# Down projection of a two-layer MLP: Strassen's scheme (Winograd's form) for 14 of 16 groups

## The chip, the cores and the metric

One core of a Trainium2 chip runs the whole program. The metric is the device time of one execution in microseconds (us). The engines have their own instruction queues: TensorE (PE in the profile), VectorE (DVE), ScalarE (ACT), GpSimd (POOL) and SyncE (SP), which here only issues DMAs. They wait for each other through semaphores.

## The reference, cut to what matters

The program is one decoder layer for a prompt of 1024 tokens and 8 decode tokens, model width 1024. Only its last part is touched:

```
x1 = LN(alpha * x + m)
y  = LN(alpha * x1 + relu(x1 @ w_up)^2 @ w_down)      # w_up 1024 x 4096, w_down 4096 x 1024
```

All is float32. A product is made exact enough by splitting: each operand is a rounded high part plus a low part (what the rounding left), and a product is three matmuls, high·high + high·low + low·high.

## The kernel before, in words

**Tiling.** The 4096 hidden channels are 32 tiles of 128, taken in 16 groups of two (group g holds tiles 2g and 2g+1; the prediction counts groups 0 to 15). The *up* half of a group has six chunks, three for each tile: a chunk is 344 tokens wide and takes 8 contraction tiles by 3 matmuls, 24 matmuls of 344 columns (`up`, line 1590; all go through `split_product`, line 902). ScalarE applies the relu of a chunk out of one of four PSUM banks (`relu`, L1958). VectorE squares it (L2636). ScalarE writes the high part (L1984), VectorE the low part (L2643).

**The down half.** `down(g)` (line 1623) runs over 8 token tiles and 2 halves of the 1024 output columns. Each of these 16 sums takes 2 hidden tiles by 3 matmuls of 512 columns and goes to one of three PSUM banks (5 to 7). VectorE adds each sum to `x1` in SBUF (L2672). The sum with number d may start when the add of sum d-3 is done. So a group has 96 such matmuls and 16 adds. The weights of a group, 256 x 1024, come by one DMA of 1 MB (L878) into a double buffer; ScalarE makes their high part (L1998) and VectorE their low part (L2703). The 8 decode tokens have their own small product, `down_decode` (L1619).

**Order.** It is written out by hand for each engine. TensorE, for groups 1 to 14: six up chunks of group g, and then the whole down half of group g-1. Group 15 has its up chunks alone; `down_last` then takes the down halves of groups 14 and 15 together, and the final layer norm runs tile by tile beside it. ScalarE and VectorE go through relu, square, high part, low part, adds, and the split of the next up weights (L920 on ScalarE, L926 on VectorE) in a fixed order. GpSimd does nothing from the merge of the branches to the final layer norm, where it applies gain and bias (L2870, L2872).

Of the kernel before, what the change touches and what calls it, by code (L numbers as in the profile page):

```python
# [28 lines left out]
P = 128  # L29
# [4 lines left out]
NB = 8  # L34
# [130 lines left out]
def hybrid_step(nc, x_p, x_s, c_cmp, c_sel, c_win, state, table, w_in, cmp_w, cmp_pos, lb_logits, norm_g,  # L165
                w_br_a, w_br_b, w_out, ln1_g, ln1_b, w_up, w_down, ln2_g, ln2_b, consts, kpos, dbias, before_d,
                y_p, y_s_out, cmp_p, sel_p, win_p, hg_p, cmp_s, sel_s, win_s, hg_s):
    with ExitStack() as ctx:
# [496 lines left out]
        uT = [aT[:, :, :].rearrange("p (j s) t -> p j s t", s=2), view(0, 2, 2, T)]  # L665
        uR = [rounded("hidden0", aT_at, 0, 2, 2, T), rounded("hidden1", arena_at, 0, 2, 2, T)]
        NG = F_FF // (2 * P)
        LAST = [(0, (NG - 2,)), (1, (NG - 2,)), (2, (NG - 2, NG - 1)), (0, (NG - 1,)), (3, (NG - 2, NG - 1)), (1, (NG - 1,))]
# [3 lines left out]
        def last_sum(e, half):  # L672

            return 16 * (NG - 2) + 2 * e + half

# [23 lines left out]
        y_s, y_g, y_out = sem("y_ready_dve"), sem("y_ready_pool"), sem("y_stored")  # L699
        l2_f, l2_g = sem("ln2_factors"), sem("ln2_gained")  # L700
# [54 lines left out]
        def _(sp):  # L755
# [117 lines left out]
            for g in range(NG):  # L873
                if g == 0:
                    sp.wait_ge(f_ps, NQ + 1)
                if g >= 2:
                    sp.wait_ge(dn_ps, 16 * (g - 1))
                sp.dma_start(wdn[:, g % 2], w_down[0, 2 * P * g:2 * P * (g + 1), :].rearrange("(j p) c -> p j c", p=P)  # L878
                             ).then_inc(wd_in[g % 2], 16)
                if g == 0:  # L880
                    sp.wait_ge(x1_s, NQ + 1)
                    sp.dma_start(lng[:, 0, :], ln2_g.to_broadcast([P, D])).then_inc(ln2_in, 16)
                    sp.dma_start(lng[:, 1, :], ln2_b.to_broadcast([P, D])).then_inc(ln2_in, 16)
                for n in range(U_U + WR + 2 * g, U_U + WR + 2 * (g + 1)):
                    if n < len(units):
                        load_unit(n)
            for p, t in enumerate(LN2_ORDER[:NQ]):
                sp.wait_ge(y_g, p + 1)
                dst = y_p[0, P * t:P * (t + 1), :] if t < NQ else y_s_out[:, 0, :]
                sp.dma_start(dst, x1[0:toks(t), t, :]).then_inc(y_out, 16)  # L890
# [73 lines left out]
        def _(pe):  # L964
# [649 lines left out]
            def down_decode(g):  # L1614
                pe.wait_ge(wd_in[g % 2], 16 * (g // 2 + 1))
                pe.wait_ge(sqd_dve, 2 * (g + 1))
                for c in range(4):
                    j, cols = c // 2, slice(512 * (c % 2), 512 * (c % 2 + 1))
                    mm = pe.matmul(PS[32 * c:32 * c + NB, 4, :], ud[:, g % 2, j, :], wdn[:, g % 2, j, cols],  # L1619
# [3 lines left out]
            def down(g):  # L1623
                pe.wait_ge(wdl_dve, g + 1)
                pe.wait_ge(ul_dve, MIXED + 2 * (g + 1))
                u, w = uR[g % 2], wdl[:, g % 2]
                for t in range(NQ):
                    tk = slice(P * t, P * t + P)
                    for half in range(2):
                        d, cols = 16 * g + 2 * t + half, slice(512 * half, 512 * (half + 1))  # L1630
                        if d >= 3:
                            pe.wait_ge(dn_dve, d - 2)
                        split_product(pe, PS[:, 5 + d % 3, :], [u[:, j, 1, tk] for j in range(2)],
                                      [u[:, j, 0, tk] for j in range(2)], [wdh[:, j, cols] for j in range(2)],
                                      [w[:, j, cols] for j in range(2)]).then_inc(dn_ps, 1)
                    if t == 1:
                        down_decode(g + 1)

            def down_last():
                for e, (t, gs) in enumerate(LAST):  # L1640
                    tk = slice(P * t, P * t + P)
                    pe.wait_ge(wdl_dve, gs[-1] + 1)
                    pe.wait_ge(ul_dve, MIXED + 2 * (gs[-1] + 1))
                    gj = [(g, j) for g in gs for j in range(2)]
                    for half in range(2):
                        d, cols = last_sum(e, half), slice(512 * half, 512 * (half + 1))
                        pe.wait_ge(dn_dve, d - 2)
                        split_product(pe, PS[:, 5 + d % 3, :], [uR[g % 2][:, j, 1, tk] for g, j in gj],
                                      [uR[g % 2][:, j, 0, tk] for g, j in gj], [down_high(g, j)[:, cols] for g, j in gj],
# [15 lines left out]
        def _(act):  # L1665
# [288 lines left out]
            def relu(y):  # L1954
# [3 lines left out]
                act.activation(uT[i // 2 % 2][:, i % 2, 0, c0:c0 + cn], PS[:, (y + 2) % 4, 0:cn], ACT.Relu).then_inc(relu_act, 1)  # L1958
# [15 lines left out]
            for i in range(F_FF // P):  # L1974
                g = i // 2
                if g >= 2:
                    act.wait_ge(dn_ps, 16 * (g - 1))
                for y in range(max(3, up_chunks(i - 1)) if i else 3, up_chunks(i)):
                    relu(y)
                if i == 0:  # L1980
                    act.wait_ge(*unit_done(U_U))
                    split_high(act, U_U + 2, up_high(2))
                act.wait_ge(sq_dve, i + 1)
                act.activation(uR[g % 2][:, i % 2, 1, 0:SEQ], uT[g % 2][:, i % 2, 0, 0:SEQ], ACT.Copy).then_inc(uh_act, 1)  # L1984
                if 1 <= i < F_FF // P - 2:
# [914 lines left out]
```

## Time and profile before

| | us |
|---|---|
| median of 3 runs | 2127.62 (2126.48 to 2130.12) |
| the profiled execution's own time | 2127.94 |
| its span | 2126.1 |
| TensorE busy | 2078.1 (98%) |
| VectorE busy | 1039.2 (49%) |
| ScalarE busy | 687.1 (32%) |
| GpSimd busy | 179.6 (8%) |

The span is what the profiler saw between the first and the last instruction; the time of an execution is a little longer. Matmuls are pipelined: in the timeline the start-to-start distance of two matmuls is what TensorE spends on one, not the length shown. The MLP's groups 1 to 15 and the last sums fill the stretch from 1398.6 us to the end.

### The profile page before, as it was taken

To read this page: it belongs to the slowest core of one execution; us is meant where nothing else is said; L and a number is where in the kernel's file an instruction comes from. 1 tells how busy PE (TensorE), PEld (TensorE's weight loads), DVE (VectorE), ACT (ScalarE), POOL (GpSimd) and SP (SyncE) were. 2 spreads that over 40 slices of the span, in tenths; PEclk is the share of its full clock that TensorE was granted. 3 is DMA by queue.
4 is the path that set the end of the run, shared out by engine and by line. 5 is a ranking of instruction groups with operands and counts; after the bars stand their busy time and mean duration, and the time that the engine had idled before them with its cause. 6 is when DMAs were issued, how large, how long until landed. Compare 5 with 4: busy or idle time off the path is not lost.

```text
span 2126.1 us, 33610 instructions
## 1 busy us (share of the span) xinstructions
PE 2078.1 (98%) x14172; PEld 1808.9 (85%) x14172; DVE 1039.2 (49%) x1915; ACT 687.1 (32%) x1345; POOL 179.6 (8%) x180
## 2 busy tenths in 40 slices
PE   8999999999999999999999999999999999999997
PEld 8997777779589999998888876898889888898985
DVE  2126777656633686675111127744434444444447
ACT  3127777755223444452111130121112111122122
POOL 0011000011500222130000000000000000000007
PEclk9999999999999999999999999999999999999999
DMA  9323010247742222123111131121111111111102
GB/s 222 121 66 115 11 51 2 90 157 248 245 153 51 56 62 56 46 65 122 30 50 40 45 114 48 47 75 40 54 46 50 45 45 41 40 60 50 30 20 80
DMA packets 140738, 159.05 MB, mean 75 GB/s; under 512 B 25843, under 2 KB 122444, under 8 KB 135725
## 3 DMA queue, kind: packets, MB, share of 16 engines
q1 hardware_dynamic: 132556, 114.14, 17.6%
q0 software_dynamic: 8032, 42.78, 6.5%
q8 instruction: 112, 1.84, 0.3%
q14 instruction: 38, 0.30, 0.0%
HBM read 141.32 MB, written 19.76 MB: 76 GB/s over the span
## 4 chain that ended last, share of the span: by engine, by line
PE 92%; DVE 3%; ACT 2%; DMA 1%; issue 1%; SPq 0%; POOL 0%; DVEq 0%; ACTq 0%; POOLq 0%
PE PS L902 64%; PE PS L1525 5%; PE PS L1136 3%; PE PS L1116 3%; PE PS L1224 3%; PE PS L1088 2%; PE PS L1090 1%; PE PS L1209 1%; PE PS L1451 1%; PE PS L1619 1%; DMA arena<-in_x_prompt 1%; PE PS L1145 1%; PE PS L1579 1%; PE PS L1394 1%; PE PS L1337 1%
## 5 line engine op out<-in xcount | busy, mean ns | idle before, releaser
L902 PE MATMUL PS<-x_low,w_high_mlp 128*128 128x344 f32 x1056 | 337.7, 320 | 0.0
L902 PE MATMUL PS<-w_down_high,hidden 128*128 128x512 f32 x960 | 308.2, 395 | 0.9 <-DVE w_down_low L2678 0.9
L902 PE MATMUL PS<-x_high,w_low 128*128 128x344 f32 x768 | 245.8, 320 | 0.0
L2672 DVE TENSOR_TENSOR arena<-arena,PS 128x512 f32<-128x512 f32 x244 | 167.4, 687 | 134.9 <-PE PS L902 134.7
L902 PE MATMUL PS<-x_high,w_high_mlp 128*128 128x344 f32 x720 | 229.8, 319 | 0.0
L902 PEld LDWEIGHTS PS<-w_down_high,hidden 128*128 128x128 f32 x960 | 180.0, 188 | 54.3 <-DVE arena L2672 12.0
L902 PE MATMUL PS<-w_down_low,hidden 128*128 128x512 f32 x512 | 200.9, 392 | 0.0
L902 PEld LDWEIGHTS PS<-x_low,w_high_mlp 128*128 128x128 f32 x1056 | 198.2, 188 | 2.6
L902 PE MATMUL PS<-x_low,w_high_hgrn 128*128 128x344 f32 x600 | 191.8, 320 | 0.0
L902 PE MATMUL PS<-x_high_a,w_low 128*128 128x344 f32 x480 | 153.5, 320 | 0.0
L902 PE MATMUL PS<-x_high_b,w_low 128*128 128x344 f32 x468 | 149.6, 320 | 0.0
L902 PEld LDWEIGHTS PS<-x_high,w_low 128*128 128x128 f32 x768 | 144.2, 188 | 0.0
L902 PEld LDWEIGHTS PS<-x_high,w_high_mlp 128*128 128x128 f32 x720 | 135.4, 188 | 1.5 <-issue 0.9
L1680 ACT ACTIVATE arena<-PS 128x344 f32<-128x344 f32 (+1 forms) x105 | 47.9, 458 | 262.4 <-PE PS L902 262.2
L1998 ACT ACTIVATE w_down_high<-arena 128x2048 fp32r<-128x2048 f32 x15 | 28.7, 1916 | 274.9 <-PE PS L902 274.9
L1525 PE MATMUL PS<-arena,wring 128*128 128x344 f32 x384 | 114.7, 452 | 1.2 <-issue 1.2
L902 PEld LDWEIGHTS PS<-w_down_low,hidden 128*128 128x128 f32 x512 | 96.1, 188 | 21.1
L902 PEld LDWEIGHTS PS<-x_low,w_high_hgrn 128*128 128x128 f32 x600 | 113.1, 189 | 0.0
L2870 POOL TENSOR_TENSOR arena<-arena 128x1024 f32<-128x1024 f32 (+1 forms) x8 | 19.6, 2451 | 1103.2 <-ACT arena L2010 1103.2
L926 DVE TENSOR_TENSOR w_low<-wring,w_high_mlp 128x1024 fp32r<-128x1024 f32 x44 | 53.6, 1220 | 109.0 <-ACT w_high_mlp L920 109.0
L1525 PEld LDWEIGHTS PS<-arena,wring 128*128 128x128 f32 x384 | 72.1, 190 | 35.1 <-issue 1.4
L902 PE MATMUL PS<-x_high_a,w_high_hgrn 128*128 128x344 f32 x300 | 101.3, 338 | 0.3 <-issue 0.3
(399 smaller groups left out, 4236.4 us busy)
## 6 DMA issues: line engine op xcount, KB each, us to landing
wring<-in_w_in SPq DMA_DIRECT2D x100, 256.0 KB, 3.3
wring<-in_w_up SPq DMA_DIRECT2D x64, 256.0 KB, 3.3
arena<-in_w_down SPq DMA_DIRECT2D x16, 1024.0 KB, 5.0
arena<-in_x_prompt SPq DMA_DIRECT2D x16, 512.0 KB, 3.6
x_high_kept<-x_high_att SPq DMA_DIRECT2D x1, 4128.0 KB, 13.9
arena<-in_w_out SPq DMA_DIRECT2D x2, 2048.0 KB, 9.6
out<-in_cache_win_kv SPq DMA_DIRECT2D x1, 4088.0 KB
out<-arena SPq DMA_DIRECT2D x7, 512.0 KB
```

The lines of the kernel that those rows point to most:

```text
L902: mm = pe.matmul(out, w, x, start=(start and k == 0 and i == 0), stop=(stop and k == tiles - 1 and i == 2))
L926: dve.tensor_tensor(wl[:, n % WR, :, 0:m], wring[:, n % WR, :, 0:m], high[:, :, 0:m].bitcast(F32), ALU.subtract).then_inc(wl_dve, 1)
L1088: pe.matmul(out, qa, k1[g][:, br, k0:k0 + n], start=True, stop=False)
L1090: mm = pe.matmul(out, qb, k2[br][g][0:65, k0:k0 + n], start=False, stop=True)
L1116: mm = pe.transpose(PS[0:n, 4 + turned % 2, P * b:P * (b + 1)], probs(j, col, n), ident)
L1136: mm = pe.matmul(PS[HD * two:HD * (two + 1), 6 + i % 2, c:c + P], v[0:r, :], PT[(2 * n + two) % 3][0:r, b // 4, P * (b % 4):P * (b % 4 + 1 ...
L1145: mm = pe.transpose(PS[:, 6 + n % 2, P * a:P * (a + 1)], out_parts(n)[:, P * a:P * (a + 1)], ident)
L1224: mm = pe.matmul(PS[:, 4 + 2 * (b % 2) + c, 0:256], cw2[:, c, 4 * half + q, :], xt2[:, n % 2, 256 * (4 * c + q):256 * (4 * c + q + 1)], st ...
L1525: mm = pe.matmul(PS[:, product_bank(s, ab), 0:cn], wring[:, n % WR, 4 * ab + k, :], a[:, k, c0:c0 + cn], start=(k == 0), stop=(k == 3))
L1680: act.activation(dst[0:m, c0:c0 + cn], unit_out(3 * n + ci, m, cn), fn).then_inc(u_act, 1)
L1998: act.activation(wdh[:, :, :], wdn[:, g % 2], ACT.Copy).then_inc(wdh_act, 1)
L2672: dve.tensor_tensor(y, y, PS[:, 5 + d % 3, :], ALU.add).then_inc(dn_dve, 1)
```

## The change

For groups 0 to 13 (`NS` = 14) the down half is computed in 2 x 2 blocks. Token tiles p and p+4 form a pair (p = 0 to 3); the blocks of the left operand are (tile p or p+4) by (hidden tile 2g or 2g+1), those of the right operand (hidden tile) by (512 output columns). Winograd's form of Strassen's scheme needs seven products of blocks instead of eight, and sums of blocks on both sides. For each pair there are four sums of squares of hidden blocks (128 x 128 elements each), for each group four sums of weight blocks (128 x 512 each). GpSimd computes them: 20 `tensor_tensor` instructions a group, in the order pairs 0, 1, 2, weights, pair 3.

A product is three matmuls of 512 columns, so a pair has 21 and a group 84. Four of the seven products have a bank of their own start; the other three (`False` in `PRODUCTS`) go on accumulating in the bank of the product three before, after that one has been added. Each of the seven is added to `x1` by VectorE: six adds of 512 elements a row, and one that adds the same sum to both halves (1024 elements).

TensorE's order in groups 1 to 14: up chunks 0 and 1, the decode product, chunk 2, pair 0 of group g-1, chunk 3, pair 1, chunk 4, pair 2, chunk 5, pair 3. The high and low parts are made of the blocks and of their sums (896 elements a row for a pair, 1536 for the weight blocks, twice 1024 for the weight sums). The buffers are single: relu output, weight parts and weight sums are not double-buffered. The weights of groups 1 to 13 are fetched when the sums, the low parts and the decode product of the group before are done. Groups 14 and 15 are computed as before, with their high parts written after the last Strassen product; the decode product of group 14 moves from the down half in group 14 to group 15, and the loads of the second layer norm's gain and bias from the start of the MLP to before the weights of group 14.

```
+        PRODUCTS = ((1, 0, True), (3, 2, True), (4, 3, True), (6, 4, False), (2, 5, True), (7, 1, False), (5, 6, False))
...
             for g in range(NG):
                 if g == 0:
-                    sp.wait_ge(f_ps, NQ + 1)
-                if g >= 2:
-                    sp.wait_ge(dn_ps, 16 * (g - 1))
...
+                elif g <= NS:
+                    sp.wait_ge(y_g, 4 * g)
+                    sp.wait_ge(wdl_dve, 3 * (g - 1) + 1)
+                    sp.wait_ge(dd_ps, g)
...
+            def down(g, p):
+                pe.wait_ge(ul_dve, MIXED + 4 * g + p + 1)
+                for m, (a, b, first) in enumerate(PRODUCTS):
+                    d = product(g, p, m)
+                    if p == 0 and m in (0, 2, 4):
+                        pe.wait_ge(wdl_dve, 3 * g + m // 2 + 1)
+                    if d >= 3:
+                        pe.wait_ge(dn_dve, d - 2)
+                    for i, (h, w) in enumerate(((hp_high[p][:, a - 1, :], wp_high[:, b, :]), (hp_high[p][:, a - 1, :], part_low(b)),
+                                                (hp_low[p][:, a, :], wp_high[:, b, :]))):
+                        mm = pe.matmul(PS[:, 5 + d % 3, :], h, w, start=(first and i == 0), stop=(i == 2), skip_group_check=True)
+                    mm.then_inc(dn_ps, 1)
...
             for g in range(NG):
                 if g >= 1:
-                    for y in range(6 * g, 6 * g + 6):
-                        up(y)
-                        if y == 8:
-                            down_decode(0)
-                if 1 <= g < NG - 1:
-                    down(g - 1)
+                    for c in range(6):
+                        up(6 * g + c)
+                        if c == 1 and g <= NS or c == 2 and g == NG - 1:
+                            down_decode(g - 1)
+                        if c >= 2 and g <= NS:
+                            down(g - 1, c - 2)
...
+            for g in range(1, NS + 1):            # ScalarE
+                quarters_high(g - 1)
+                parts_high(g - 1, 0)
+                sums_high(g - 1, 0)
+                relu(6 * g)
+                parts_high(g - 1, 1)
+                sums_high(g - 1, 1)
+                parts_high(g - 1, 2)
+                relu(6 * g + 1)
+                parts_high(g - 1, 3)
+                relu(6 * g + 2)
+                up_split(2 * g + 2)
+                for c in range(3, 6):
+                    relu(6 * g + c)
+                up_split(2 * g + 3)
...
+            def square_quarters(g, p):
+
+                dve.wait_ge(relu_act, up_chunks(2 * g + 1))
+                if g:
+                    dve.wait_ge(dn_ps, product(g - 1, p, 7))
...
+            for g in range(1, NS + 1):            # VectorE
+                if g >= 2:
+                    square_quarters(g - 1, 3)
+                quarters_low(g - 1)
+                parts_low(g - 1, 0)
+                sums_low(g - 1, 0)
+                sums_low(g - 1, 1)
+                parts_low(g - 1, 1)
+                if g >= 2:
+                    weights_low(2 * g + 1)
+                parts_low(g - 1, 2)
+                square_decode(2 * g)
+                add_pair(g - 1, 0)
+                weights_low(2 * g + 2)
+                parts_low(g - 1, 3)
...
+                add_pair(g - 1, 1)
+                add_pair(g - 1, 2)
+                square_decode(2 * g + 1)
...
+                    for p in range(3):
+                        square_quarters(g, p)
+                add_pair(g - 1, 3)
...
+            def hidden_sums(g, p):
+                pool.wait_ge(sq_dve, 4 * g + p + 1)
+                h, n = hp_raw[p], 4 * (4 * g + p)
+                pool.tensor_tensor(h[:, 5, :], h[:, 1, :], h[:, 0, :], ALU.subtract).then_inc(l2_g, 1)
+                pool.tensor_tensor(h[:, 4, :], h[:, 0, :], h[:, 2, :], ALU.add).then_inc(l2_g, 1)
+                pool.wait_ge(l2_g, n + 1)
+                pool.tensor_tensor(h[:, 6, :], h[:, 2, :], h[:, 5, :], ALU.subtract).then_inc(l2_g, 1)
+                pool.wait_ge(l2_g, n + 3)
+                pool.tensor_tensor(h[:, 7, :], h[:, 3, :], h[:, 6, :], ALU.subtract).then_inc(l2_g, 1)
+
+            def weight_sums(g):
+                pool.wait_ge(wd_in[g % 2], 16 * (g // 2 + 1))
+                if g:
+                    pool.wait_ge(dn_ps, product(g, 0, 0))
...
```

The comments `# ScalarE` and `# VectorE` are added here. `weight_sums` holds four subtractions of 512 elements a row; the second waits for the first, the third for the second.

## Rows read from the trace of the kernel before

**Rows 1.** The page's first part: busy us of each engine, share, instructions.

```profile
PE 2078.1 (98%) x14172; PEld 1808.9 (85%) x14172; DVE 1039.2 (49%) x1915; ACT 687.1 (32%) x1345; POOL 179.6 (8%) x180
```

**Rows 2.** The chain of waits: start us, length us, what; one decode product.

```profile
1842.23 0.97 PE PS L1619 x8
```

**Rows 3.** Timeline of TensorE: start us, length, line, out<-in; first matmuls of stretches.

```profile
1398.57 0.32 PE L902 MATMUL PS<-x_high,w_high_mlp 128*128 128x344 f32 x1
...
1445.70 0.32 PE L902 MATMUL PS<-x_high,w_high_mlp 128*128 128x344 f32 x1
...
1859.92 0.32 PE L902 MATMUL PS<-x_high,w_high_mlp 128*128 128x344 f32 x1
...
1882.60 0.39 PE L902 MATMUL PS<-w_down_high,hidden 128*128 128x512 f32 x1
...
1905.87 0.32 PE L902 MATMUL PS<-x_high,w_high_mlp 128*128 128x344 f32 x1
...
2043.98 0.32 PE L902 MATMUL PS<-x_high,w_high_mlp 128*128 128x344 f32 x1
```

**Rows 4.** Groups by line and shape, 1658 to 2026 us: count | busy us, mean ns.

```profile
L2672 DVE TENSOR_TENSOR arena<-arena,PS 128x512 f32<-128x512 f32 x128 | 87.9, 687 | 73.1 <-PE PS L902 73.1
L926 DVE TENSOR_TENSOR w_low<-wring,w_high_mlp 128x1024 fp32r<-128x1024 f32 x16 | 19.5, 1219 | 0.0
...
L920 ACT ACTIVATE w_high_mlp<-wring 128x1024 fp32r<-128x1024 f32 x16 | 16.7, 1043 | 0.0
```

**Rows 5.** Timeline of VectorE: other sizes, and two adds back to back.

```profile
1332.44 1.08 DVE L2536 TENSOR_TENSOR x_high<-arena,x_low 128x896 fp32r<-128x896 f32 x1
...
1337.30 1.22 DVE L2599 SCALAR_TENSOR_TENSOR arena<-arena,PS 128x1024 f32<-128x1024 f32 x1 [3.78 <-PE PS L902]
...
2070.85 1.28 DVE L2672 TENSOR_TENSOR arena<-arena,PS 128x512 f32<-128x512 f32 x2
```

**Rows 6.** Timeline, and one piece of the chain: hand-overs between engines.

```profile
1860.12 0.69 DVE L2672 TENSOR_TENSOR arena<-arena,PS 128x512 f32<-128x512 f32 x1 [0.70 <-PE PS L902]
1860.17 1.92 ACT L1998 ACTIVATE w_down_high<-arena 128x2048 fp32r<-128x2048 f32 x1 [19.71 <-PE PS L902]
...
1882.79 0.46 ACT L1958 ACTIVATE arena<-PS 128x344 f32<-128x344 f32 x1 [3.32 <-PE PS L902]
1883.29 1.23 DVE L2636 TENSOR_TENSOR arena<-arena 128x1024 f32<-128x1024 f32 x1 [6.63 <-ACT arena L1958]
...
2074.41 0.04 issue
```

**Rows 7.** Timelines of VectorE and GpSimd, 918 to 923 us.

```profile
918.42 1.23 DVE L926 TENSOR_TENSOR w_low<-wring,w_high_hgrn 128x1024 fp32r<-128x1024 f32 x1
918.48 1.65 POOL L2846 TENSOR_TENSOR consts_sb<-consts_sb,arena 128x256 f32<-128x256 f32 x1 [4.95 <-DVE arena L2449]
...
920.67 1.04 POOL L2848 TENSOR_TENSOR consts_sb<-consts_sb,arena 128x512 f32<-128x512 f32 x1
920.81 1.44 DVE L2458 TENSOR_TENSOR arena<-arena 128x512 f32<-128x512 f32 x1
921.85 1.00 POOL L2853 TENSOR_TENSOR consts_sb<-consts_sb 128x256 f32<-128x256 f32 x1
```

**Rows 8.** The end: the chain's pieces on VectorE, GpSimd's timeline beside them.

```profile
2113.73 0.70 DVE arena L2672
2113.88 2.34 POOL L2872 TENSOR_TENSOR arena<-arena 128x1024 f32<-128x1024 f32 x1
2115.43 1.35 DVE arena L2736
2116.18 2.79 POOL L2870 TENSOR_TENSOR arena<-arena 128x1024 f32<-128x1024 f32 x1
2116.81 2.72 DVE arena L2736
```

**Rows 9.** The page's DMA issues: transfers, KB each, us to landing.

```profile
arena<-in_w_down SPq DMA_DIRECT2D x16, 1024.0 KB, 5.0
```

More of the change, by code:

```diff
@@ L672, in last_sum @@
         def last_sum(e, half):
-            return 16 * (NG - 2) + 2 * e + half
+            return product(NS, 0, 0) + 2 * e + half
         U_M = len(units)
@@ L1617, in down_decode @@
                 for c in range(4):
-                    j, cols = c // 2, slice(512 * (c % 2), 512 * (c % 2 + 1))
-                    mm = pe.matmul(PS[32 * c:32 * c + NB, 4, :], ud[:, g % 2, j, :], wdn[:, g % 2, j, cols],
+                    j, half = c // 2, c % 2
+                    rows = wd_raw[:, c, :] if g < NS else wdn[:, g % 2, j, 512 * half:512 * (half + 1)]
+                    mm = pe.matmul(PS[32 * c:32 * c + NB, 4, :], ud[:, g % 2, j, :], rows,
                                    start=(g == 0), stop=(g == NG - 1), skip_group_check=True)
                 mm.then_inc(dd_ps, 1)
[L1623 to L1637, printed above, removed]
+            def down(g, p):
[10 more added lines that the diff above has]
+                    mm.then_inc(dn_ps, 1)
             def down_last():
@@ new lines, in up_split, with hidden_high @@
+            def up_split(i):
+                act.wait_ge(*unit_done(U_U + i - 2))
+                split_high(act, U_U + i, up_high(i))
+            def hidden_high(i):
+                act.wait_ge(sq_dve, 4 * NS + i - 2 * NS + 1)
+                act.wait_ge(dn_ps, product(NS, 0, 0))
+                raw, _, high = hidden_last[i // 2 % 2]
+                act.activation(high[:, i % 2, 0:SEQ], raw[:, i % 2, 0:SEQ], ACT.Copy).then_inc(uh_act, 1)
+            relu(3)
+            relu(4)
+            up_split(2)
@@ new lines, in _ @@
+            relu(5)
+            up_split(3)
+            for g in range(1, NS + 1):
[13 more added lines that the diff above has]
+                up_split(2 * g + 3)
@@ new lines, in _ @@
+            for i in range(2 * NS, 2 * NS + 2):
+                hidden_high(i)
+            act.wait_ge(wd_in[NS % 2], 16 * (NS // 2 + 1))
+            act.activation(wdh[:, :, :], wdn[:, NS % 2], ACT.Copy).then_inc(wdh_act, 1)
+            for c in range(3):
+                relu(6 * (NG - 1) + c)
+            act.wait_ge(wd_in[(NG - 1) % 2], 16 * ((NG - 1) // 2 + 1))
+            for j in range(2):
+                ins = act.activation(wdhL[j][:, :], wdn[:, (NG - 1) % 2, j], ACT.Copy)
+            ins.then_inc(wdh_act, 1)
@@ L1999, in _ @@
+            hidden_high(F_FF // P - 2)
+            for c in range(3, 6):
+                relu(6 * (NG - 1) + c)
+            hidden_high(F_FF // P - 1)
             for p, t in enumerate(LN2_ORDER):
```

200 lines of the change are left out of this document (131 added, 69 removed).

## The prediction

> **What bounds the kernel now.** I read the busy shares first: TensorE has 98% of the span, VectorE 49%, GpSimd 8% [rows 1]. Then the chain of waits over the MLP: it is TensorE's matmuls without a break, only cut by a decode product of 0.97 us in each group [rows 2]. So an engine other than TensorE sets no time there, and what TensorE spends is the time. Its timeline gives the prices [rows 3]. Groups 2 to 14 begin at 1445.70 and group 15 at 2043.98: 46.02 us a group. Group 1, which has two decode products, takes 1445.70 - 1398.57 = 47.13. Within one group the six up chunks take 1882.60 - 1859.92 = 22.68 (3.78 each), the down half 1905.87 - 1882.60 = 23.27; less 0.98 for the decode product, 22.29 for 96 matmuls, so 0.232 each.
>
> **What is removed.** A pair has 21 matmuls in place of 24, a group 84 in place of 96: 12 x 0.232 = 2.79 us. A group of TensorE work alone is then 22.68 + 0.98 + 84 x 0.232 = 43.16, 2.86 under today's (the odd 0.07 is small waits). With no stall anywhere, groups 1 to 14 would give back about 40 us. The question is what TensorE comes to wait for.
>
> **What is added on VectorE.** An add of 512 costs 0.687 and a 1024-wide subtraction 1.219 [rows 4], so 1.04 ns an element beside a fixed part; 896 elements took 1.08, and 1024 out of PSUM 1.22 [rows 5]. 1536 elements, which no row shows, lie on that line at 1.75. Two adds back to back took 1.28 together [rows 5]: the next starts 0.1 before the last ends, an add every 0.59. The busy sum of a group: 24 adds at 0.59 and 4 wide ones at 1.12 make 18.6, the squares, low parts and weight splits about 12.8, so 31 of 47 us. VectorE is no bound by its sum; its order and its neighbour matter. Within a pair a product takes 3 x 0.232 = 0.697, an add 0.59: adds keep up once they are on time. But product 3 of a pair (counted from 0) waits for add 0 by the three banks, where today a sum takes 1.39 us: the slack is 2.09 us after the pair's start, half of before. Whatever stands ahead of add 0 on VectorE beyond that is a stall.
>
> **What is added on GpSimd, and what it takes from VectorE.** 20 two-input instructions on SBUF a group. The trace has both engines at such work at once [rows 7]. At 920.67 GpSimd runs 1.04 us, to 921.71. VectorE's square of 512 elements (both inputs one SBUF tensor, as in the new squares) starts at 920.81 and takes 1.44, not 0.69: it ends 0.54 after GpSimd does. GpSimd's next, started at 921.85, ends at 922.85, 0.60 after VectorE's end. At 918.42 VectorE was first, and GpSimd's 256 elements took 1.65. The end of the kernel shows the same with 1024 elements [rows 8]: VectorE asks at 2115.43 and ends 0.56 after GpSimd's 2116.22; GpSimd, asking at 2116.18, ends 2.19 after that; VectorE, asking at 2116.81, ends at 2119.53, 0.56 after GpSimd. So the two never overlap, and the one that waits goes next. An add that reads PSUM is not touched: 0.70 beside a running GpSimd [rows 8].
>
> The time that each holds the other off: VectorE 0.54 for 512 elements, 0.93 for 896, 1.07 for 1024, 1.60 for 1536 (by 1.04 ns). GpSimd 0.60 for 256 and 2.19 for 1024, thus 0.07 + 2.07 ns an element: 0.33 for the 128 of a hidden sum, 1.13 for the 512 of a weight sum. Neither size stands in the trace with two full inputs. The bounds: from 20% less (the 512-element row of 1.04 us has a repeated second operand) to 16% more (the 128-element one costs as two thirds of 256).
>
> The Trainium skill (SBUF — State Buffer, SBUF: two separate sides) says that the shared port pair is an exclusive lock, held for the whole instruction by whichever came first. The rows agree on the exclusion but not on "whole": a waiting VectorE instruction ends 0.54 after the release, not its full 0.69. By the page's reading each of the 16 turns below would cost about 0.14 more, 2.3 us a group.
>
> **Timetable of a steady group**, zero when TensorE has ended the last product of the group before. Hand-overs [rows 6]: matmul to add 0.20 (1860.12 after the next matmul's start at 1859.92), matmul to relu 0.28, relu 0.46, ScalarE to VectorE 0.04 (1882.79 to 1883.29), VectorE to TensorE 0.04. The wide add ends at 1.42, VectorE is free at 1.34. GpSimd still has the third pair's hidden sums to do, whose squares came late in the group before, to 1.6. ScalarE's weight high part runs from 0.25 to 1.74 (1.92 for 2048 [rows 6], 1.04 for 1024 [rows 4]). The port then passes from one to the other: square of pair 3 (to 2.1), weight sum 1 (3.2), low part of the weight blocks (4.8), sum 2 (6.0), low part of pair 0 (6.9), sums 3 and 4 (9.3), low parts of the weight sums with the first of pair 3's hidden sums between (11.7), then hidden sum, pair 1 (13.0), hidden sum, up weights (14.4), hidden sum, pair 2 (15.7). As a sum: VectorE 0.54 + 1.60 + 3 x 0.93 + 3 x 1.07 = 8.1, GpSimd 4 x 1.13 + 4 x 0.33 = 5.8, from 1.6: 15.6. Pair 3's last hidden sum is ready at 14.7; its high part (0.93) stands on ScalarE ahead of the third relu, and VectorE's decode square waits for that relu: 16.1. Add 0 of pair 0 runs 16.2 to 16.9. TensorE reaches pair 0 at 3 x 3.78 + 0.98 = 12.32 and product 3 at 14.41; it may start at 16.93. **First stall: 2.5 us.**
>
> Second place: chunk 5 ends at U, its relu at U + 0.74. VectorE does the decode square and the three squares of the next group before it adds pair 3's sums: squares to U + 1.5 and U + 2.1, one hidden sum takes its turn (0.33), the third square to U + 3.0. Add 0 ends at U + 3.6, product 3 wanted to start at U + 2.09. **Second stall: 1.6 us**, of which 1.3 stay without GpSimd. Pairs 1 and 2 have a whole chunk (3.78) of VectorE's time ahead of them and less than that before them: none. The three products behind a late one wait 0.04 to 0.05 each, 0.1 in all.
>
> A group: 43.16 + 2.5 + 1.6 + 0.1 = 47.4, 1.35 over today's; 13 groups (2 to 14) make **+17.5**. Group 1: its four squares, the third up split and all 16 hidden sums begin only after the last relu of group 0, 0.9 after its start: VectorE's holds 9.7 and GpSimd's 16 x 0.33 + 4 x 1.13 = 9.8, with some 2.5 of gaps where GpSimd's chain waits for itself, bring add 0 to about 23.5 instead of 16.2. So 54.8 against 47.13: **+7.7**. The decode product moved into group 15: **+1.0**. The sum is +26.2, on the profiled execution's 2127.94: 2154.1; that execution lies 0.3 above the median.
>
> **Costed at nothing.** SP: the weights of group g are asked for at about 9.3 of a group (last weight sum) and land 5.0 later [rows 9]; they are needed at 47, so 33 us cover them; the up weights queued behind wait for TensorE's chunk 2 (12.3) anyway. Groups 14 and 15's weights are asked for at the start of group 15 and land by 10, before the decode product at 11.3. Their high parts, low parts and the relus fit in the 22.7 us of group 15; without that cover the price would be the 1.9 + 2.3 of a weight split. The layer norm loads move to an idle queue. ScalarE has some 12 us of work in 47. For the clock nothing is charged: stalls of 2.5 us cover 5% of a stretch; if it fell, every term would grow.
>
> **Rivals.**
> A. The two engines do not get in each other's way here. For it: the new operands are other regions, and many of VectorE's instructions have none of GpSimd's beside them. Against: every one of the overlaps in [rows 7, 8]. Then GpSimd's work ends before TensorE's pair 0, the first stall is gone and the second is 1.3: 44.5 a group, 13 x -1.49 = -19.4, group 1 +0.6, decode +1.0: **2110**. This is the faster side; it decides once the port's turns end before 13.1, the first add's earliest start.
> B. As forecast, but GpSimd's turns are 20% shorter (0.27 and 0.91): the first stall falls to about 0.7, a group takes 45.5; -6 + 6 + 1: **2129**, no change.
> C. VectorE keeps the port while its instructions follow back to back, or the holds are whole instructions: GpSimd's sums come later, and with them the third relu. The first stall grows to 4.8 to 5.0: 49.7 a group, **2186**. No row has two such VectorE instructions in a row against a waiting GpSimd. The skill's whole-instruction rule gives 2154 + 14 x 2.3 = 2186 too.
> D. No stall at all: 13 x -2.86, group 1 -4.0, decode +1.0: **2088**. Against: the second stall follows from the order on VectorE alone.
>
> **Chances.** The forecast 0.50 (own range 2138 to 2175), A 0.16, B 0.14, C 0.15, D 0.05. What can be told from no change is about 0.2%, 4 us. Faster: A, D and a third of B, 0.26. Same: 0.04. Slower: the forecast, C and the rest of B, 0.70. The range of 2106 to 2182 leaves out D and most of C.
>
> **What would show it.** Right: TensorE's busy share in the middle of the MLP near 91% (43.2 of 47.4) instead of 100%, groups 47.4 apart, two gaps a group behind product 2 of pairs 0 and 3, of 2.5 and 1.6, both ended by VectorE's add; VectorE's two-input instructions in the first 16 us at two to three times their 1.08 to 1.22; weight sums on GpSimd of 1.3 alone and up to 2.9 where they wait; the third relu at 15 to 16 of a group. Wrong: low parts at their old lengths beside running sums (A), gaps at other products or before pair 1, or waits of pair 0 for its low parts, which the timetable has ready at 6.9 (hidden), 10.3 and 11.7 (weight sums), against products at 12.3, 13.7 and 15.1: 3.4 us of cover, and each us beyond it would come on top.

## The result, and the profile after

| | before | after |
|---|---|---|
| median of 4 runs, us | 2128.11 (2126.48 to 2130.12) | 2162.89 (2160.3 to 2166.17) |
| profiled execution, us | 2127.94 | 2161.19 |
| its span, us | 2126.1 | 2159.4 |

The change makes the kernel slower: ratio 1.0163, 95% interval 1.0151 to 1.0175. The forecast was 2154, with a range of 2106 to 2182. The profiled execution is 33.3 us longer, where the sum said 26.2.

The page after, parts 1 and 4, answers to [rows 1, 2]:

```profile
span 2159.4 us, 34210 instructions
PE 2058.8 (95%) x14004; PEld 1779.5 (82%) x14004; DVE 1299.4 (60%) x2167; ACT 724.8 (34%) x1401; POOL 448.2 (21%) x460
...
PE 77%; POOL 13%; DVE 4%; ACT 2%; issue 2%; DMA 1%; SPq 0%; DVEq 0%; POOLq 0%; ACTq 0%
```

TensorE is busy 19.3 us less than before, although 14 x 2.79 = 39 us of its matmuls are gone: the rest came back in the page's way of counting: slower matmuls in stretches of lower clock (below), matmuls before a gap, which count at full length, and waits of 0.1 us or less behind late adds, which the modelled lengths hide. And it waits besides. 13% of the chain that ended last is now GpSimd's, which did not stand in the MLP's chain before. The waits of TensorE from 1400 to 2070 (us in total, times, longest):

```profile
PE PS L1668 <- DVE arena L2789: 47.5, 27, 4.7
PE PS L1668 <- DVE w_down_sums_low L2730: 3.7, 1, 3.7
```

27 waits for an add: two in each of groups 1 to 13, and one in group 14, whose gap at pair 3 (only 0.54) lies behind 2070. Its timeline shows where they are (a bracket: idle time before, and what ended it), and answers to [rows 3]:

```profile
1456.75 0.32 PE L936 MATMUL PS<-x_high,w_high_mlp 128*128 128x344 f32 x1
...
1551.98 0.32 PE L936 MATMUL PS<-x_high,w_high_mlp 128*128 128x344 f32 x1
...
1564.50 0.39 PE L1668 MATMUL PS<-w_down_parts_high,hidden_parts_high 128*128 128x512 f32 x1
...
1568.71 0.50 PE L1668 MATMUL PS<-w_down_parts_high,hidden_parts_high 128*128 128x512 f32 x1 [1.95 <-DVE arena L2789]
...
1571.76 0.32 PE L936 MATMUL PS<-x_high,w_high_mlp 128*128 128x344 f32 x1
...
1592.86 0.39 PE L1668 MATMUL PS<-w_down_parts_high,hidden_parts_high 128*128 128x512 f32 x1
...
1596.44 0.50 PE L1668 MATMUL PS<-w_down_parts_high,hidden_parts_high 128*128 128x512 f32 x1 [1.32 <-DVE arena L2789]
...
1599.43 0.32 PE L936 MATMUL PS<-x_high,w_high_mlp 128*128 128x344 f32 x1
...
2075.97 0.32 PE L936 MATMUL PS<-x_high,w_high_mlp 128*128 128x344 f32 x1
```

The group from 1551.98 to 1599.43 takes 47.45. Pair 0 begins 12.52 after its start and takes 1571.76 - 1564.50 = 7.26; 21 matmuls at 0.232 are 4.87. From pair 0's start to product 3, 4.21 pass instead of 9 x 0.232 = 2.09: a gap of 2.1. In pair 3, 1596.44 - 1592.86 = 3.58, a gap of 1.5.

The chain that ended last, of after, from the last pieces of the group before to product 3 (start, us, piece):

```profile
1553.22 1.26 POOL consts_sb L3019
...
1554.56 1.64 POOL consts_sb L3021
...
1556.26 2.69 POOL consts_sb L3023
1558.95 2.09 POOL consts_sb L3024
1561.04 1.41 POOL aT L3007
1562.45 1.40 POOL aT L3008
1563.86 1.28 POOL aT L3010
...
1565.20 1.33 POOL aT L3012
...
1566.56 0.03 ACT hidden_parts_high L2014
...
1567.41 0.45 ACT aT L1994
...
1567.89 0.04 DVE arena L2707
...
1567.97 0.69 DVE arena L2789
```

This shows the first gap's chain in one view (pieces called "issue" are left out). GpSimd's four weight sums and pair 3's four hidden sums end at 1566.5. ScalarE makes the high part of pair 3 (0.95 in its own timeline; the chain's piece is only its start) and only then runs the third relu at 1567.41. VectorE's decode square waits for that relu, and the first add of pair 0 stands behind the square at 1567.97. A hidden sum of 128 elements takes 0.42 to 0.47 alone and 1.28 to 1.41 here, where VectorE's low parts take turns with it. VectorE's groups in the same group of the MLP (busy us, mean ns, idle time before):

```profile
L2720 DVE TENSOR_TENSOR hidden_parts_low<-arena,hidden_parts_high 128x896 fp32r<-128x896 f32 x3 | 4.9, 1623 | 0.0
L2730 DVE TENSOR_TENSOR w_down_sums_low<-consts_sb,w_down_parts_high 128x1024 fp32r<-128x1024 f32 x2 | 3.7, 1829 | 0.0
L2725 DVE TENSOR_TENSOR w_down_quarters_low<-arena,w_down_parts_high 128x1536 fp32r<-128x1536 f32 x1 | 2.9, 2855 | 0.0
```

896 elements take 1.62 on average, not 1.08 [rows 5], and 1536 take 2.86. Two of these instructions in VectorE's timeline:

```profile
1554.95 2.85 DVE L2725 TENSOR_TENSOR w_down_quarters_low<-arena,w_down_parts_high 128x1536 fp32r<-128x1536 f32 x1
1557.72 2.18 DVE L2720 TENSOR_TENSOR hidden_parts_low<-arena,hidden_parts_high 128x896 fp32r<-128x896 f32 x1
```

The first ends at 1557.80, 1.60 after GpSimd's sum of L3021 (1556.20); the second ends at 1559.90, 0.95 after that of L3023 (1558.95). The forecast's holds for these sizes were 1.60 and 0.93. The idle time before them all is 0.0: VectorE waited for no result of GpSimd in this stretch until the third relu (0.42). Its queue from the square of pair 3 (1553.32) to the last low part (1567.47) took 14.2 us; the same queue takes 9.3 in the second run of experiment 1 (1536.32 to 1545.61). So at least 4.9 us are the lengthened instructions.

**Where the 33.3 us are.** The windows give the whole stretch of groups 2 to 14 and single pieces (us, then the busy time of PE, PEld, DVE, ACT, POOL; granted clock; DMA share; GB/s). After:

```profile
1456.75:2075.97 619.22, 577.41 (x3070) 499.86 (x3068) 508.37 (x559) 148.13 (x195) 243.42 (x251) 0.99 0.14 43
1551.98:1599.43 47.45, 44.18 (x238) 38.26 (x236) 39.07 (x44) 11.39 (x15) 19.10 (x21) 1.00 0.15 45
1711.00:1715.00 4.00, 3.94 (x10) 3.13 (x11) 2.67 (x5) 0.15 (x1) 0.00 (x0) 0.57 0.00 0
1418.00:1429.00 11.00, 5.92 (x15) 4.25 (x16) 8.03 (x11) 3.74 (x6) 4.47 (x4) 0.55 0.46 143
960.00:965.00 5.00, 5.00 (x54) 4.88 (x51) 2.53 (x7) 2.06 (x4) 0.00 (x0) 0.53 0.01 3
```

Before:

```profile
1445.70:2043.98 598.28, 598.28 (x3225) 529.44 (x3224) 264.58 (x325) 112.98 (x143) 0.00 (x0) 1.00 0.14 45
960.00:965.00 5.00, 5.00 (x65) 4.93 (x61) 3.04 (x9) 2.07 (x4) 0.00 (x0) 1.00 0.02 5
```

Groups 2 to 14: 619.22 - 598.28 = +20.9. Group 1: 1456.75 - 1400.56 = 56.2 against 47.13, +9.1. From group 15 to the end: 83.4 against 82.1, +1.3. The start of group 1 is +2.0, in code that the change doesn't touch: around 960 TensorE ran at its lower level of 1.2 GHz in this execution (granted clock 0.53) and at 2.4 GHz in the one of before, which made it 3 us late; 1 us of that was gone again by group 1. Together 33.3.

### The profile page after: what moved, and what is told of

The parts are those of the page before. It is cut to its first block, busy times and chain, and to the rows that moved or that the text cites. A ratio compares the mean times of both kernels' runs of the same rounds, so it can differ in the third digit from the quotient of the medians.

```text
span 2159.4 us, 34210 instructions
## 1 busy us (share of the span) xinstructions
PE 2058.8 (95%) x14004; PEld 1779.5 (82%) x14004; DVE 1299.4 (60%) x2167; ACT 724.8 (34%) x1401; POOL 448.2 (21%) x460
## 4 chain that ended last, share of the span: by engine, by line
PE 77%; POOL 13%; DVE 4%; ACT 2%; issue 2%; DMA 1%; SPq 0%; DVEq 0%; POOLq 0%; ACTq 0%
PE PS L936 41%; PE PS L1668 9%; PE PS L1559 5%; PE PS L1170 3%; PE PS L1150 3%; PE PS L1258 3%; POOL consts_sb L3023 2%; PE PS L1122 2%; PE PS L1124 1%; POOL consts_sb L3024 1%; PE PS L1243 1%; POOL arena L3007 1%; POOL arena L3008 1%; POOL consts_sb L3021 1%; POOL arena L3012 1%
## 5 line engine op out<-in xcount | busy, mean ns | idle before, releaser
L2789 DVE TENSOR_TENSOR arena<-arena,PS 128x512 f32<-128x512 f32 x336 | 221.2, 686 | 70.6 <-PE PS L1668 63.7
L1668 PE MATMUL PS<-w_down_parts_high,hidden_parts_high 128*128 128x512 f32 x392 | 162.3, 414 | 51.6 <-DVE arena L2789 47.8
L3007 POOL TENSOR_TENSOR arena<-arena 128x128 f32<-128x128 f32 x42 | 26.3, 625 | 786.8 <-DVE arena L2715 786.8
L1994 ACT ACTIVATE aT<-PS 128x344 f32<-128x344 f32 x90 | 40.4, 449 | 348.4 <-PE PS L936 348.4
L1668 PE MATMUL PS<-w_down_parts_high,hidden_parts_low 128*128 128x512 f32 x392 | 156.3, 399 | 0.0
L936 PEld LDWEIGHTS PS<-x_high,w_high_mlp 128*128 128x128 f32 x720 | 135.3, 188 | 15.4 <-issue 12.9
L1668 PEld LDWEIGHTS PS<-w_down_parts_high,hidden_parts_high 128*128 128x128 f32 x392 | 74.7, 191 | 85.2 <-DVE arena L2789 64.0
L936 PE MATMUL PS<-x_high_b,w_high_hgrn 128*128 128x344 f32 x300 | 99.9, 333 | 0.0
```

The source lines that it names most:

```text
L936: mm = pe.matmul(out, w, x, start=(start and k == 0 and i == 0), stop=(stop and k == tiles - 1 and i == 2))
L1668: mm = pe.matmul(PS[:, 5 + d % 3, :], h, w, start=(first and i == 0), stop=(i == 2), skip_group_check=True)
L2789: ins = dve.tensor_tensor(y, y, sums, ALU.subtract if m == 4 else ALU.add)
L3007: pool.tensor_tensor(h[:, 5, :], h[:, 1, :], h[:, 0, :], ALU.subtract).then_inc(l2_g, 1)
```

## The experiments

Medians are compared with runs of the kernel before on the same chip (2129.07, 2130.43 or 2127.95). "A group" is the steady distance of group starts in the MLP.

**1. Does GpSimd hold VectorE off at all, and by its reads?** The sums were replaced by fills of the same places: GpSimd writes, and reads nothing. The sums are left out of the computation.

```
-pool.tensor_tensor(h[:, 5, :], h[:, 1, :], h[:, 0, :], ALU.subtract).then_inc(l2_g, 1)
+pool.memset(h[:, 5, :], 0.0).then_inc(l2_g, 1)      # and so for all eight sums
```

> The changed kernel with each of GpSimd's 20 sums a group replaced by one fill of the same tile (it writes zeros and reads nothing; waits and counts stay), so the sums are left out of the computation. Theory P (VectorE's two-input instructions and GpSimd's sums keep each other off, and the late adds stall TensorE): VectorE's low parts fall back to 1.09 (896 elements) and 1.22 (1024), the gap behind product 2 of pair 0 goes, the one of pair 3 shrinks from 1.5 to about 1.3 us; a group takes 44.5 instead of 47.45, group 1 about 48 instead of 56.2: 2163 - 13 x 2.9 - 8 = 2117 (2111 to 2123), faster than the kernel before. Rival O (it is only the order and the sum of VectorE's own work; GpSimd merely runs beside it): both gaps stay, 2158 or more.

Measured: 2112.89, ratio 0.9928 (0.9901 to 0.9955); a group 44.80, no gap at pair 0, one of 1.22 at pair 3. GpSimd's fills (busy us, mean ns):

```profile
L3010 POOL MEMSET arena<- 128x128 f32 x42 | 8.6, 205 | 0.0
...
L3019 POOL MEMSET consts_sb<- 128x512 f32 x14 | 7.4, 527 | 37.8 <-PE PS L1668 37.8
```

They are half as long as sums, so a second version filled in pieces (4 x 32 and 8 x 64 elements). It was meant to keep GpSimd busy as long as a real sum does alone.

```
+for c in range(8):
+    ins = pool.memset(w[:, 0, 64 * c:64 * (c + 1)], 0.0)
+ins.then_inc(y_g, 1)
```

> As the kernel with fills, but every hidden sum is now four fills of 32 elements and every weight sum eight of 64, so that GpSimd is busy about as long as an undisturbed sum keeps it (about 0.5 us in place of 0.46, and 1.2 in place of 1.29), still without reading anything; the sums are left out of the computation. It tells whether VectorE is held off by GpSimd's reading or by any GpSimd instruction, and whether the time at which the results come matters. Theory P (reading, two inputs against two inputs): as with the short fills, low parts at 1.09 and 1.22, no gap at pair 0: 2113 to 2116. Rival K (any running GpSimd instruction holds VectorE's two-input work off, or the sums simply come too late): the gap at pair 0 is back, at 1.5 to 2.1 us: 2140 to 2160.

Measured: 2111.63, ratio 0.992 (0.99 to 0.9941), 1 us under its range, a group again 44.80. GpSimd's timeline, VectorE's beside it, and VectorE's means in two MLP groups:

```profile
1535.27 0.76 POOL L3028 MEMSET consts_sb<- 128x64 f32 x8 [1.76 <-PE PS L1668]
...
1537.59 0.76 POOL L3039 MEMSET consts_sb<- 128x64 f32 x8
1538.28 0.30 POOL L3008 MEMSET aT<- 128x32 f32 x4
```

```profile
1536.92 1.75 DVE L2725 TENSOR_TENSOR w_down_quarters_low<-arena,w_down_parts_high 128x1536 fp32r<-128x1536 f32 x1
```

```profile
L2720 DVE TENSOR_TENSOR hidden_parts_low<-arena,hidden_parts_high 128x896 fp32r<-128x896 f32 x6 | 6.5, 1083 | 0.0
L2725 DVE TENSOR_TENSOR w_down_quarters_low<-arena,w_down_parts_high 128x1536 fp32r<-128x1536 f32 x2 | 3.5, 1752 | 0.0
```

The fills are not as long as was meant: eight of 64 elements run in 0.76 together and four of 32 in 0.30, against 1.27 and 0.46 for a sum alone, because the next one starts before the last has ended. So what GpSimd's lateness does by itself was not tested by this run. What it does show is the other half: from 1535.27 on, GpSimd fills nearly without a break for 4 us, and VectorE's low parts right beside it are back at 1.08 and 1.75. A GpSimd that only writes does not hold VectorE off; one that reads two SBUF inputs does. Whether one input would be enough was not tried. Together it is about 47.45 - 44.80 = 2.65 us a group, and rival A's world gives 2112 against its 2110. The rule of the Trainium skill (SBUF — State Buffer, Who interferes with whom), that a VectorE instruction with two SBUF inputs contends with a GpSimd instruction that reads SBUF and not with one that only writes, agrees with both runs.

**2. Is it the relu behind pair 3's high part?** On ScalarE the third relu was put before that high part.

```
-                parts_high(g - 1, 3)
                 relu(6 * g + 2)
+                parts_high(g - 1, 3)
```

> One part of the order undone: ScalarE does the third relu of a group before the high part of pair 3, not after it. Theory P: in the trace after, VectorE is done with pair 2's low part 0.4 us before the third relu ends; with the relu early the decode square and the adds start 0.4 to 0.5 sooner, the first gap falls from 2.1 to about 1.6 and the rest stays: 13 x 0.5 = 6.5 and 1 to 2 in group 1: 2155 (2151 to 2159). Rival L (the stall is GpSimd's chain of results on ScalarE's path, not the port): the whole first gap goes with the relu out of that chain: 2163 - 13 x 2.3 - 5 = 2128.

Measured: 2150.26, ratio 1.0102 (1.0074 to 1.0129); a group 46.93, gaps of 1.59 and 1.49. The first gap lost 0.5, and rival L's 2128 is excluded. It wasn't the relu alone: VectorE's own low parts, the last at 15.5 of a group in the trace of after, end almost as late. The time is 1 us under the expected range: the clock, which fell in two groups of after, fell in none of groups 2 to 14 here.

**3. And with the weight sums off GpSimd?** They were moved to VectorE, each where its operands are ready; the hidden sums stay on GpSimd.

```
+                weight_sum(g - 1, 0)
                 if g >= 2:
                     square_quarters(g - 1, 3)
+                weight_sum(g - 1, 1)
                 quarters_low(g - 1)
+                weight_sum(g - 1, 2)
+                weight_sum(g - 1, 3)
                 parts_low(g - 1, 0)
```

> The four weight sums of a group are made by VectorE instead of GpSimd (the first two around the square of pair 3, the last two after the low part of the weight blocks). VectorE gets 4 x 0.6 = 2.4 us more work in exactly the stretch that is late. Theory P: the port's turns lose 4 x 1.13 and gain 4 x 0.54, 14.0 becomes 11.6; from 1.3 they end at about 13, the first add starts in time, the first gap goes and the second (1.5) stays: 44.9 a group, group 1 about 5 less: 2163 - 13 x 2.5 - 5 = 2125 (2118 to 2132). Rival O (VectorE's own load is what is late): 2.4 us more in front of the first add makes the first gap 4.5: 2163 + 13 x 2.4 = 2194.

Measured: 2122.57 (10 runs), ratio 0.9971 (0.9959 to 0.9984); a group 45.08, no gap at pair 0, 1.48 at pair 3. Though VectorE has 4 x 0.69 = 2.8 us more to do in a group, TensorE no longer waits for it in pair 0 of the steady groups (group 1 still has one gap there, of 6.0): on GpSimd the same four took 7.8 us (1553.22 to 1561.04 in the chain above). This one edit turns the slowdown into a gain of 0.3%. The second gap stays as it was, so it isn't the weight sums' doing.

**4. Both, and one square taken out of the way of pair 3's adds.** The edits of experiments 2 and 3 are both in, and the square of pair 0 goes before pair 2's adds, where VectorE has time; it waits only for the relu of chunk 4. Against experiment 3, without the relu:

```
+                if g < NS:
+                    square_quarters(g, 0)
                 add_pair(g - 1, 2)
...
-                    for p in range(3):
+                    for p in range(1, 3):
                         square_quarters(g, p)
```

> The kernel with the weight sums on VectorE, and two changes of order: the third relu ahead of pair 3's high part, and the square of pair 0 moved from in front of pair 3's adds to in front of pair 2's (it needs only the relu of chunk 4). Theory P: one square less (0.6, and a GpSimd turn less behind it) in front of pair 3's adds: the gap behind its product 2 falls from 1.48 to about 0.7; 45.08 a group becomes 44.2, group 1 about 3 less: 2122.6 - 13 x 0.85 - 3 = 2109 (2104 to 2114). Rival G (GpSimd's work moved into the first stretch comes back there as a gap of pair 0): no gain, 2120 or more.

Measured: 2114.81, ratio 0.9924 (0.9905 to 0.9943); a group 44.35, the gap at pair 3 down from 1.48 to 0.62. The squares in front of pair 3's adds in experiment 3 (first line) and here (second):

```profile
1492.65 2.15 DVE L2715 TENSOR_TENSOR arena<-aT 128x512 f32<-128x512 f32 x3
1492.53 1.29 DVE L2715 TENSOR_TENSOR arena<-aT 128x512 f32<-128x512 f32 x2
```

A square that left the front of the adds gave back 0.86: 0.60, its own step in the queue, and 0.26 of waiting for GpSimd's first hidden sum. Of it 0.14 is lost again in pair 2, whose adds the moved square now makes a little late (5.03 instead of 4.89). The time is 1 us above the expected range; group 1 gained 1.7, not 3. What the relu gave here was not measured by itself.

**5. The other way to empty that place: pair 3's adds before all squares of the next group.**

```
                 square_decode(2 * g + 1)
+                add_pair(g - 1, 3)
...
-                add_pair(g - 1, 3)
```

> The changed kernel with all seven adds of pair 3 ahead of the three squares of the next group on VectorE: the late add of the second gap is undone by itself. Theory P: the gap behind product 2 of pair 3 (1.48) goes, but the squares then stand in the stretch that is late already, and GpSimd's first twelve hidden sums with them (12 x 0.33 + 3 x 0.54 + hand-overs, some 6.5 to 7 us later): the first gap grows from 2.1 to 8 to 9; 47.45 a group becomes 52.7: 2163 + 13 x 5.2 = 2231 (2215 to 2240). Rival S (each gap stands for itself): 2163 - 13 x 1.5 = 2143.

Measured: 2250.16 (2 runs), ratio 1.0566 (1.0545 to 1.0587); a group 54.6, more than the 52.7 expected and 10 us over its range in all. The gap at pair 3 is gone, and pair 0 has two:

```profile
1636.37 0.50 PE L1668 MATMUL PS<-w_down_parts_high,hidden_parts_high 128*128 128x512 f32 x1 [3.16 <-DVE w_down_sums_low L2730]
...
1642.87 0.80 PE L1668 MATMUL PS<-w_down_parts_high,hidden_parts_high 128*128 128x512 f32 x1 [5.32 <-DVE arena L2789]
```

The adds follow TensorE's products one by one, so the squares behind them start a whole pair later; GpSimd's 12 hidden sums, its weight sums and the low parts of the next group all start later with them. 1.5 us were saved at pair 3, and a group became 54.6 - 47.45 = 7.1 longer. After the second gap the clock was at 0.58 too (1643 to 1648), which the expectation hadn't charged.

**6. How much are seven products of eight worth, with nothing else?** The kernel before, with one of eight quarter products left out in groups 0 to 13 and no sums (a part of the result is missing).

```
+                        js = range(1 if t >= 4 and half else 2)
-                        split_product(..., [u[:, j, 1, tk] for j in range(2)], ...
+                        split_product(..., [u[:, j, 1, tk] for j in js], ...
```

> The kernel before with one of the eight quarter products of every pair of token tiles left out in groups 0 to 13 (3 matmuls of a sum of 6), nothing else changed: TensorE's saving alone, without Strassen's sums, without one more add. Both theories: 14 x 12 x 0.232 = 39 us off 2128: 2089 (2087 to 2092). If it is less, the saved matmuls were not on the path and the term of 2.79 a group in the forecast was wrong.

Measured: 2090.78, ratio 0.9819 (0.9791 to 0.9846). The window shows TensorE without a break:

```profile
1500.00:2000.00 500.00, 500.00 (x2729) 444.17 (x2728) 235.73 (x290) 101.48 (x129) 0.00 (x0) 1.00 0.15 47
```

So 38 us are there to be had, a group at about 43.3.

**7. A version for that: the low parts spread out.** On top of experiment 4, the low parts of pairs 1 to 3 go behind the adds of pairs 0 and 1, and the square of pair 2 behind the adds of pair 3.

```
-                parts_low(g - 1, 1)
...
-                parts_low(g - 1, 2)
...
                 add_pair(g - 1, 0)
+                parts_low(g - 1, 1)
                 weights_low(2 * g + 2)
-                parts_low(g - 1, 3)
...
                 add_pair(g - 1, 1)
+                parts_low(g - 1, 2)
+                parts_low(g - 1, 3)
...
-                    for p in range(1, 3):
-                        square_quarters(g, p)
+                    square_quarters(g, 1)
                 add_pair(g - 1, 3)
+                if g < NS:
+                    square_quarters(g, 2)
```

> As the last kernel, and the rest of VectorE's work put where nothing waits for it: the low parts of pair 1 behind pair 0's adds, those of pairs 2 and 3 behind pair 1's, the square of pair 2 behind pair 3's adds. The arithmetic is the same. Theory P: add 0 of pair 3 is in time to 0.1, and the first stretch has 8.1 - 1.9 of low parts, 2.2 of weight sums, 1.1 of squares, and GpSimd's 8 to 9 turns of 0.33, which end before 13: no gap over 0.3 is left, a group is TensorE's own 43.2 to 43.5, group 1 about 5 less than with the sums on VectorE: 2122.6 - 13 x 1.7 - 5 = 2096 (2091 to 2103), 1.5% under the kernel before. Rival G: what is moved only shows up as a gap before pair 1 or 2: 2109 or more.

Measured: 2103.26, ratio 0.9873 (0.9856 to 0.9889), the fastest that computes the whole layer: 1.3% under the kernel before, and 0.9873 / 1.0163 = 0.971 of the changed one (each against the kernel before on its own chip). Groups 2 to 14 of it:

```profile
1449.85:2018.92 569.07, 568.69 (x3069) 497.50 (x3068) 495.21 (x612) 148.18 (x195) 156.10 (x200) 1.00 0.15 47
```

569.07 / 13 = 43.77 a group, 0.4 us of idle time in 13 groups. It misses the expected time by 7 us and stands just outside its range. 5 of the 7 are 13 groups of 43.77 in place of about 43.4: pairs 2 and 3 take 5.03 and 5.11 and not 4.87, by waits of 0.1 behind adds that are only just in time. The other 2 are the start of group 1, at 1402.91 here and at 1400.83 in experiment 3, in code that no edit touched.

**8. Is it the order, or the engine of the weight sums?** The same order with the weight sums back on GpSimd.

> The same order as the last kernel, but the four weight sums on GpSimd as in the changed kernel. Theory P: the pair 3 gap goes as there, but GpSimd's 4 x 1.13 stay in the first stretch against VectorE's 4 x 0.54: a gap behind product 2 of pair 0 of 2 to 2.5 us stays, 45.8 a group: 2163 - 13 x 1.6 - 6 = 2135 (2128 to 2141), still not faster than before. Rival O (all is order): it is as fast as the one with the sums on VectorE, about 2096.

Measured: 2157.09, ratio 1.0124 (1.0103 to 1.0144); a group 47.7. That is 16 us above the expected range, although the gap came out as expected: the one at pair 3 is gone, the one at pair 0 is 2.17. Behind it the clock falls in every group, which the expectation had not charged:

```profile
1515.43 0.51 PE L1668 MATMUL PS<-w_down_parts_high,hidden_parts_high 128*128 128x512 f32 x1 [2.00 <-DVE arena L2789]
...
1516.94 0.63 PE L1668 MATMUL PS<-w_down_sums_low,hidden_parts_high 128*128 128x512 f32 x1
1517.37 0.63 PE L1668 MATMUL PS<-w_down_parts_high,hidden_parts_low 128*128 128x512 f32 x1
```

```profile
1515.40:1518.40 3.00, 2.97 (x8) 2.25 (x9) 2.33 (x4) 1.82 (x2) 0.00 (x0) 0.58 0.45 127
```

The two matmuls are 0.43 apart, the granted clock of the stretch is 0.58. Pair 0 takes 8.7 to 8.9 in the groups from 2 on, where 4.87 and the gap and its small waits make 7.3: some 1.5 us a group, about 20 in all, is the clock. VectorE has work it could do, but its queue is in order: it stands at the low parts of the weight sums (view of VectorE's groups, last column idle time before them):

```profile
L2730 DVE TENSOR_TENSOR w_down_sums_low<-consts_sb,w_down_parts_high 128x1024 fp32r<-128x1024 f32 x2 | 3.6, 1794 | 5.0 <-POOL consts_sb L3026 4.9
```

4.9 us of waiting for GpSimd's third weight sum. Here GpSimd's lateness itself stalls VectorE, beside the time for which the two hold each other off. In the same order, the engine of four sums a group makes 2157 or 2103. What the order alone gives is hidden by the clock: with the sums on GpSimd it takes 1.5 us out of pair 3 and the clock takes 1.5 back in pair 0.

## Why the prediction was right, and where its sizes were off

**The mechanism held.** Two gaps in a group, behind product 2 of pairs 0 and 3, both ended by VectorE's add, and none elsewhere in the steady groups. The first place hangs on what its chain said: third relu at 15.4 to 15.9 of a group (forecast 15 to 16), first add of pair 0 at 16.0 (16.2), pair 0 itself at 12.52 (12.32). Experiments 1 and 3 take this gap away from either side, GpSimd's reads or the weight sums in its queue; experiment 2 shortens it by the relu. One of the signs was put too high: VectorE's instructions of the first 16 us were not all at two to three times their length but at 1.2 to 2.5 times; the turns add up to the forecast time all the same (the last low part ends at 15.5, forecast 15.7).

**Terms of a group**, forecast and measured:

| | forecast | measured |
|---|---|---|
| TensorE without the two gaps | 43.16 | 43.85 |
| first gap | 2.5 | 2.1 |
| second gap | 1.6 (1.3 without GpSimd) | 1.48 (1.22 in experiment 1) |
| small waits in late pairs | 0.1 | in the first row |
| a group | 47.4 | 47.45 |

The total came out better than its parts: that 47.45 meets 47.4 to 0.1 is luck. The stall of pair 0 was sized 0.4 too long, 0.2 because the first add is that much earlier and 0.2 because TensorE reaches pair 0 that much later. TensorE's own part was 0.7 too short: 0.2 in the chunks beside the decode product, up to pair 0 (12.52 for 12.32), and 0.5 behind the two gaps (0.27 in pair 0, 0.21 in pair 3), where the forecast had 0.1 for small waits. The price of a matmul was right: pairs that wait for nothing take 4.86 to 4.89, as 21 x 0.232. The forecast of a busy share near 91% is met by starts (43.85 of 47.45 is 92%); the page's way of counting gives 44.18 of 47.45, 93%, since the matmul before a gap counts at its full length.

**The clock was the term left out.** "For the clock nothing is charged": in two of the 13 groups, the ones that begin at 1694.33 and 1885.61, TensorE's clock fell to its lower level behind the first gap (0.57 from 1711 to 1715), and these groups took 48.83 and 48.85, 1.4 more. That is 2.8 of the 20.9. The other 18.1 stand against the forecast 17.5. With what group 1 and the start lost to it (below), the clock makes some 7 us of the 33.3, which is nearly the whole distance to the forecast 26.2.

**Group 1** was +9.1 against +7.7. Its timeline has two gaps in pair 0, of 3.9 (ended by the low part of the weight sums, L2730) and 5.1 (by the add), not one; that the products would wait for low parts stood among the signs of being wrong, as what would come on top, and in this one group it did. From 1418 to 1429 the clock was 0.55 and matmuls 0.425 apart. Pair 0 took 15.99; less its 4.87 and the two gaps, an estimate of 2.1 is left for slow matmuls. Without it group 1 would be at +7.0, and the two gaps (9.0) are less than the one stall of 9.8 in the sum. So here a stall sized too long and a clock left out offset each other in part.

**The decode product** moved to group 15: +1.3 with all of the end, against +1.0. **The start of group 1**, +2.0, is in no step of the sum; it comes from a stretch of lower clock around 960, in unchanged code. Without it and the 2.8 the profiled execution would be at 28.5 over before, and without group 1's 2.1 at about 26.4, against 26.2.

**The rivals.** A (no interference, 2110) is the world of experiment 1, 2113 and 2112, and so its price was right and its premise wrong. C (VectorE keeps the port) would have given 49.7 a group; the turns alternate as in [rows 7, 8], so its first half is excluded by the chain itself. The Trainium skill (SBUF — State Buffer, SBUF: two separate sides) says that the first gets the ports for the whole instruction and the other is blocked. The exclusion agrees; for "whole" the lengths decide: the low parts above end 1.60 and 0.95 after the release, where undisturbed ones take 1.75 and 1.08. (The totals say the same, 49.7 by whole instructions and 47.45 measured, but less surely, since errors offset each other in them.) B was mispriced: 20% off GpSimd's turns is 1.2 us, so its first stall is 1.3 and not 0.7, a group 46.1 and its time about 2136. It is excluded at either price, and so are its turns: the third weight sum ends 1.15 after VectorE's low part of the weight blocks (1557.80 to 1558.95), as the forecast's 1.13. D's price (2088) is near experiment 6's 2091; experiment 7 comes to within 12 us of it.

**Still open** is when the clock falls. Behind gaps of 2.1 us it fell in 2 of 13 groups of after; behind 2.17 in every group of experiment 8; behind 1.6 and less never in groups 2 to 14 of experiments 2 to 4. The length of the gap doesn't decide it: the gaps at 1711 and 1902 are no longer than the others of that trace (2.11), and behind its longest in these groups, 2.44 in group 2, the clock stayed at its upper level:

```profile
1473.50:1477.50 4.00, 3.69 (x17) 2.92 (x18) 3.88 (x7) 0.05 (x1) 0.00 (x0) 1.00 0.01 2
```

No run varied this alone.

## What to carry to other kernels

Before work is moved to an idle engine, look at what it shares with the busy one: 20 sums on GpSimd that read SBUF cost VectorE and the products behind it 2.65 us a group, more than nine tenths of the 2.8 that the scheme saves, and four of them on VectorE itself were cheaper than on the idle engine. A saving on the bound engine takes nothing off the others' work but shortens their deadlines (here from 4 us of slack to 2 at product 3), so list, for each bank that is reused, everything that stands ahead of its add on its in-order queue. Then spread the work that no product needs yet behind the adds, and run the bare saving first (experiment 6) to know what is there.

## What the runs showed of the hardware that was not expected

- A granted clock that falls behind a gap of only about 2 us: 0.57 and 0.58 in the windows above, matmuls of 512 columns 0.425 apart instead of 0.232, about 1.4 us lost each time; and one gap of 2.44 behind which it did not fall.
- Fills on GpSimd, even short ones that follow each other nearly without a break for 4 us, leave VectorE's two-input instructions at their lengths alone (1.083 for 896 elements, 1.752 for 1536).
- GpSimd's two-input instruction alone takes 0.42 to 0.47 for 128 elements and 1.26 to 1.29 for 512; the forecast had bounded these from 256 and 1024.
- Short fills on GpSimd overlap: four of 32 elements show 0.125 each and end after 0.30 together, eight of 64 show 0.152 each and end after 0.76. Busy times of single ones must not be added up.
